# A fused two-block network: the filter network's first steps moved ahead of the projection, and five instead of one filling product in the routing

## The chip, the cores and the metric

The kernel runs on one core of one Trainium2 chip, in one launch. The metric is the device time of the launch in microseconds; the kernel before takes 2229.22 us (median of 3 runs). TensorE multiplies, VectorE and ScalarE do the elementwise work, SyncE and ScalarE issue the DMAs.

## The reference

Two hybrid layers (attention, RWKV-7, retention, feed-forward) are followed by a second block on 256 tokens of width 1024. Only the second block is touched. What matters of it, shortened:

```
h = rms_norm(x, g_mix) * (1 + sc1) + sh1
p = h @ w_in + b_in                                  # the projection, 1024 x 3600
q, k, v, o, gates, hx = split(p)
y_m  = mlstm_mixer(q, k, v, o, gates, ...)
filt = hyena_filters(256, w1, b1, w2, b2, w3, freq, deltas)
y_h  = hyena_mixer(hx, ..., filt, ...)
x = x + gt1 * (concatenate([y_m, y_h]) @ w_out)
hf = rms_norm(x, g_ffn) * (1 + sc2) + sh2
x = x + gt2 * expert_choice_moe(hf, w_router, w_gate, w_up, w_down)   # 16 experts, 32 tokens each

def hyena_filters(L, w1, b1, w2, b2, w3, freq, deltas):
    hid = sin(freq * (z @ w1 + b1))                  # z: 256 x 33, constant; 64 hidden units
    hid = sin(freq * (hid @ w2 + b2))
    return (hid @ w3) * (exp(-t * abs(deltas)) + 0.05)
```

The filters do not depend on `x`. The experts choose their tokens by a top-k of the router's softmax; the weights of an expert are 24 MB in 12 loads of 2 MB.

## The kernel before

Each engine has its own stream of instructions, written out by hand, with waits on semaphores between them. The projection of the second block is done in 16 tiles `q`; tile `q` uses columns of ring slot `n = q // 2` (three slots, loaded by SyncE). A tile writes bank `q % 2` of the accumulator PS and is copied out by ScalarE in `proj_out` (L1280; the gate rows, tiles 4 and 5, by L1273). Tiles 0 and 1 are plain products (L783, reached through `project` and `product`). Tiles of slots 1, 3, 4 to 7 are done in three rounds of products (`split_tile`, L796, L800, L804): ScalarE makes a rounded high part of the weights (`high_weights`, L1303) and of h (L1310, the tile `xh`), VectorE the low parts (`low_weights2`, L1450, and L1456, `xl`).

The filter network runs between these tiles. TensorE's `project_beside_filters` holds: tile 0; z @ w1 (L858, `f_hid` 1); tile 1; two unread products; hid @ w2 (L862, `f_hid` 2); tile 2; then four rounds of two filter tiles (hid @ w3, L842) and one tile each (tile 3; the gate rows, L816; tile 6; tile 7); then the spectra (L851). VectorE's `sine_argument` brings an argument into range in seven linked steps (L1432 to L1442, `f_arg`), ScalarE takes the sine (L1317, `f_sin`). VectorE takes the absolute value of the deltas once (L1459, `f_abs`), ScalarE makes the windows (L1289, `f_win`), and VectorE multiplies window and filter tile (L1466, `f_filt`). A filter tile `i` may be written only when `f_filt` stands at `i - 1`.

`unread(bank, times)` (L748) is a product of a constant with a constant that nobody reads; it costs TensorE time only and writes a bank that is free there.

The loads of the filter network are issued by ScalarE: small ones (`hyw1`, `hyw2`, and others) during the last feed-forward; the constants `c2` (1.9 MB, with z in it) at the start of the second block; then `filter_loads` (w3, two halves, L1264; the deltas, 1 MB, L1265). All of them count on the one semaphore `two_loaded`; the wait ahead of L858 is for 11 loads, which is all of them.

In the routing (`route`, `first_expert`) TensorE makes the router's logits (L1041), turns them (L1056) for VectorE's top-k (L1638 to L1642, ended by the copies to L1661), meanwhile does other products and one `unread(2)`, and then waits for the top-k in `index_row` (L1074). It goes on with the indices' products (L1068), the gather of the chosen tokens (L1082), and the experts' products: `hidden` (L1093, gate and up, one per 2 MB load) and `down_products` (L1109). SyncE issues the next 2 MB load (L667) each time such a product group frees its place; from then on to the end the 16 experts' weights are streamed.

Of the kernel before, what the change touches and what calls it, by code (L numbers as in the profile page):

```python
# [33 lines left out]
T = 256  # L34
# [227 lines left out]
def build(nc, io):  # L262

    ctx = ExitStack()
    with ctx:
# [11 lines left out]
        def sem(name):  # L277
            return ctx.enter_context(nc.semaphore(name))
# [209 lines left out]
        p2 = w_(16384, P2_N)  # L488
        hyw1, hyw2 = lora[0:33, 384:448], lora[0:64, 256:384]
        ARG, TRN = lora[:, 512:768], lora[:, 768:1024]  # L490
# [100 lines left out]
        def first_slot(m):  # L591
# [19 lines left out]
         expert_slots, xs_staged, ge_ready, hs_ready, he_ready, ht_ready, ht_out, ye_ready, scattered,  # L611
         vec2, out_done, place6, place7, h2_scaled, z_conv, extra_a_full, extra_b_full, extra_c_full, rows_made, rows_taken, part_sums, xh2_ready, xl2_ready, high2_ready, low2_ready) = (S[n] for n in names2)
        BASE2 = START + LAYERS * LAYER_BLOCKS
        FULL2 = 32 * LAYERS * LAYER_SLOTS // RING
# [120 lines left out]
        def second_tensor(pe):  # L735
# [9 lines left out]
            def unread(bank, times=1):  # L745

                for _ in range(times):
                    nt.matmul(PS[:, bank, 0:T], ones, con[:, 0:T], start=True, stop=True)  # L748
# [105 lines left out]
            def project_beside_filters():  # L854

                project(0, 1, 0)
                pe.wait_ge(two_loaded, 11 * 16)
                nt.matmul(PS[0:64, 3, 0:T], hyw1, c2[0:33, D_Z:D_Z + T], start=True, stop=True).then_inc(f_hid, 1)  # L858
                project(1, 2)
                unread(5, 2)  # L860
                pe.wait_ge(f_sin, 1)
                nt.matmul(PS[:, 3, T:2 * T], hyw2, ARG[0:64, :], start=True, stop=True).then_inc(f_hid, 1)  # L862
                project(2, 3)
                pe.wait_ge(f_sin, 2)
                for n in range(4):
                    filter_tiles(2 * n, 2 * n + 2)
                    project(BESIDE_FILTERS[n], BESIDE_FILTERS[n] + 1)
                pe.wait_ge(f_sum, 2)
                filter_spectra(0, 8)
# [164 lines left out]
            def route():  # L1034
# [26 lines left out]

                unread(2)
                pe.wait_ge(tok2_out, 4)
# [167 lines left out]
            token_sums(2, SQ1[:, 0:8:7, :]).then_inc(ss2, 1)  # L1231
            unread(5)
            pe.wait_ge(sq2, 2)
# [10 lines left out]
        def second_scalar(act):  # L1244
# [51 lines left out]

            act.dma_start(c2, io["constants_2"][:, 0:D_WORK]).then_inc(two_loaded, 16)
            def high_weights(n):

                s = n % RING  # L1300
                act.wait_ge(ring_full[s], FULL2 + 32 * (n // RING + 1))
                for i in range(4):
                    ins = na.activation(HIGH2[n][i].rearrange("p k c -> p (k c)"), ring[:, s, 1024 * i:1024 * (i + 1)], ACT.Copy)  # L1303
                ins.then_inc(high2_ready, 1)

            root(1)
            shifted()
            filter_loads()
            act.wait_ge(h2_ready, KD)
# [91 lines left out]
        def second_vector(dve):  # L1401
# [25 lines left out]
            def sine_argument(n):  # L1427
# [3 lines left out]
                arg, trn = ARG[rows, :], TRN[rows, :]  # L1431
                link(nv.tensor_scalar(arg, PS[rows, 3, T * n:T * (n + 1)], p2[rows, P2_HY + n:P2_HY + n + 1], p2[rows, P2_HY + 2:P2_HY + 3], ALU.add, ALU.mult))  # L1432
                big = 1.5 * 2.0 ** 23
# [19 lines left out]
            def filters():  # L1453
                lf = LF[0:H2]
                dve.wait_ge(xh2_ready, 1)
                nv.tensor_tensor(XL2[:, :, :], hT[:, :, :], XH2[:, :, :].bitcast(F32), ALU.subtract).then_inc(xl2_ready, 1)  # L1456
                low_weights2(1)
                dve.wait_ge(two_loaded, 11 * 16)
                nv.scalar_tensor_tensor(DELTA, DELTA, -1.0, DELTA, ALU.mult, ALU.max).then_inc(f_abs, 1)  # L1459
                sine_argument(0)  # L1460
                sine_argument(1)
                for i in range(8):
                    c, t, _ = filter_tile(i)
                    dve.wait_ge(f_h, i + 1)
                    dve.wait_ge(f_win, i + 1)
                    nv.scalar_tensor_tensor(FILT[:, t, c, :], WIN[:, i % 2, :], 0.05, PS[:, 4 + i % 2, :], ALU.add, ALU.mult).then_inc(f_filt, 1)  # L1466
                    if i == 1:
                        low_weights2(3)
                    elif i == 5:
                        dve.wait_ge(act2, 6)  # L1470
                        nv.scalar_tensor_tensor(lf, G4[0:H2, 1::2, :], -1.0, G4[0:H2, 1::2, :], ALU.mult, ALU.max).then_inc(gate_rows, 1)
                        conv(QK2, 0, P2_CQW, P2_CQB, 0, 4, 8)
# [943 lines left out]
        def _(act):  # L2416
# [246 lines left out]
            act.dma_start(wrt, io["router"]).then_inc(two_loaded, 16)  # L2663
            act.dma_start(hyw1, io["hy_w1_2"][0]).then_inc(two_loaded, 16)
            for half in range(2):
                act.dma_start(hyw2[:, 64 * half:64 * half + 64], io["hy_w2_2"][0]).then_inc(two_loaded, 16)
            na.activation(bias[:, 3:4], onec, ACT.Sqrt)
# [556 lines left out]
```

## Time and profile before

| | |
|---|---|
| median of 3 runs | 2229.22 us (2229.08 to 2229.65) |
| the profiled execution | 2227.82 us |
| its span | 2225.9 us |
| TensorE products busy in the span | 1888.0 us |
| VectorE, ScalarE busy | 956.5 us, 549.9 us |
| mean granted clock of TensorE | 0.917 of 2.4 GHz |
| bytes moved | 613.15 MB, mean 275 GB/s |

The span is divided among three stretches that matter here: the projection of the second block with the filter network (about 1090 to 1232 us), the rest of the mixer and the routing (to about 1318 us), and the experts (to the end). In the rows below a time is in us from the span's start; a row of a timeline has start, busy us, engine, line, operation, tiles, count, and in brackets how long the engine had been idle and what released it. One matmul of float32 appears as two records.

### The profile page before, as it was taken

Reading aid. Unit: us, or ns where it says so; the run is one execution under the profiler, and the core shown is the slowest. Engines: PE = TensorE matmul, PEld = TensorE weight load, DVE = VectorE, ACT = ScalarE, POOL = GpSimd, SP = SyncE. Lnnn points to the kernel's source line nnn. Section 1 sums busy time; section 2 is a strip of 40 time slices with the busy share of each in tenths; the row PEclk is TensorE's granted clock in tenths of the full one; section 3 lists DMA queues with packets and bytes.
Section 4 is the critical chain, followed back from the end, with each engine's and each line's share of the span. In section 5 each row is a group of like instructions: output and inputs, shape, how many; then the busy total and the mean of one; then the engine's idle time right before and its main releaser. Section 6 shows DMA issues by size and latency. Waiting matters only on the chain.

```text
span 2225.9 us, 28935 instructions
## 1 busy us (share of the span) xinstructions
PE 1888.0 (85%) x12562; PEld 1313.9 (59%) x12562; DVE 956.5 (43%) x1334; ACT 549.9 (25%) x580; POOL 30.2 (1%) x23
## 2 busy tenths in 40 slices
PE   7999999999999999999999999566666666666675
PEld 7998788888999878888769773121121212121211
DVE  6789458666769746865567630000000000000000
ACT  4555013443364302443354111000000000000001
POOL 0000010000000000000000000000000000000000
PEclk9999999999999999999999999878788878788868
DMA  7443734657443543565643579999999999999997
GB/s 255 174 157 117 256 114 152 199 156 219 174 163 141 189 181 114 189 190 156 197 152 114 202 308 427 428 427 428 428 429 428 429 428 428 429 428 428 429 428 326
DMA packets 189554, 613.15 MB, mean 275 GB/s; under 512 B 8332, under 2 KB 105100, under 8 KB 164236
## 3 DMA queue, kind: packets, MB, share of 16 engines
q1 hardware_dynamic: 186928, 602.04, 70.0%
q10 hardware_dynamic: 2524, 9.60, 1.2%
q8 instruction: 82, 1.34, 0.2%
q14 instruction: 20, 0.16, 0.0%
HBM read 610.57 MB, written 1.05 MB: 275 GB/s over the span
## 4 chain that ended last, share of the span: by engine, by line
PE 51%; DMA 35%; DVE 9%; ACT 2%; issue 1%; SPq 0%; ACTq 0%; DVEq 0%; PEldq 0%
DMA ring<-in_w_down 11%; DMA ring<-in_w_gate 11%; PE PS L1981 10%; DMA ring<-in_w_up 10%; PE PS L1982 5%; PE PS L1093 3%; PE PS L1886 3%; PE PS L1961 3%; PE PS L1954 3%; PE PS L1956 2%; DMA work<-in_w_down 2%; DVE ring_low L2705 1%; PE PS L1109 1%; PE PS L783 1%; PE PS L1868 1%
## 5 line engine op out<-in xcount | busy, mean ns | idle before, releaser
L1093 PE MATMUL PS<-work,proj 128*32 128x512 f32 x1024 | 155.0, 738 | 96.1 <-DMA work<-in_w_up 56.9
L1694 DVE TENSOR_TENSOR proj<-proj,PS 128x512 f32<-128x512 f32 x16 | 11.0, 688 | 495.3 <-PE PS L1093 495.3
L1981 PE MATMUL PS<-x_both,high_f 128*128 128x512 f32 x608 | 210.9, 396 | 0.0
L1982 PE MATMUL PS<-x_both,ring_low 128*128 128x256 f32 x704 | 195.6, 278 | 0.0
L1093 PE MATMUL PS<-ring,proj 128*32 128x512 f32 x768 | 126.7, 793 | 79.7 <-DMA ring<-in_w_up 41.0
L2688 DVE TENSOR_TENSOR ring_low<-ring,high_f 128x4096 fp32r<-128x4096 f32 (+1 forms) x38 | 146.8, 3863 | 27.8 <-ACT high_f L2437 27.7
L1093 PEld LDWEIGHTS PS<-work,proj 128*32 128x32 f32 x1024 | 31.2, 123 | 214.5 <-DMA work<-in_w_up 95.1
L2437 ACT ACTIVATE high_f<-ring 128x4096 fp32r<-128x4096 f32 (+1 forms) x38 | 121.1, 3188 | 114.5 <-PE PS L1982 90.3
L1385 ACT ACTIVATE proj<-PS 128x512 f32<-128x512 f32 x16 | 9.6, 597 | 518.3 <-PE PS L1093 518.2
L1982 PEld LDWEIGHTS PS<-x_both,ring_low 128*128 128x128 f32 x704 | 132.3, 188 | 0.0
L1981 PEld LDWEIGHTS PS<-x_both,high_f 128*128 128x128 f32 x608 | 114.2, 188 | 26.7
L1093 PEld LDWEIGHTS PS<-ring,proj 128*32 128x32 f32 x768 | 24.5, 128 | 175.2 <-DMA ring<-in_w_up 70.7
L1698 DVE TENSOR_TENSOR proj<-PS,xT 128x512 f32<-128x512 f32 x32 | 20.7, 687 | 223.7 <-PE PS L1109 207.1
L1981 PE MATMUL PS<-hid_both,high_f 128*128 128x512 f32 x308 | 106.9, 392 | 0.0
L1954 PE MATMUL PS<-xh_a,high_a 128*128 128x256 f32 x416 | 99.8, 283 | 0.0
L1956 PE MATMUL PS<-hT_low,high_a 128*128 128x256 f32 x400 | 96.8, 281 | 0.0
L1109 PE MATMUL PS<-work,proj 128*32 128x512 f32 x448 | 67.6, 735 | 25.5 <-DMA work<-in_w_down 22.7
L1982 PE MATMUL PS<-hid_both,ring_low 128*128 128x256 f32 x308 | 85.9, 279 | 0.0
L1387 ACT ACTIVATE proj<-PS 128x512 f32<-128x512 f32 x16 | 9.6, 597 | 295.6 <-PE PS L1101 295.6
L1142 PE MATMUL PS<-proj 128*128 128x512 f32 x128 | 62.5, 632 | 22.9 <-DVE proj L1698 22.9
L1109 PE MATMUL PS<-ring,proj 128*32 128x512 f32 x352 | 57.2, 782 | 29.0 <-DMA ring<-in_w_down 29.0
L1954 PEld LDWEIGHTS PS<-xh_a,high_a 128*128 128x128 f32 x416 | 77.3, 188 | 0.3 <-issue 0.2
(565 smaller groups left out, 3695.1 us busy)
## 6 DMA issues: line engine op xcount, KB each, us to landing
ring<-in_w_in SPq DMA_DIRECT2D x73, 1024.0 KB, 7.4
work<-in_w_gate SPq DMA_DIRECT2D x32, 2048.0 KB, 35.7
work<-in_w_up SPq DMA_DIRECT2D x32, 2048.0 KB, 35.5
work<-in_w_down SPq DMA_DIRECT2D x28, 2048.0 KB, 35.8
ring<-in_w_up SPq DMA_DIRECT2D x25, 2048.0 KB, 35.4
ring<-in_w_gate SPq DMA_DIRECT2D x23, 2048.0 KB, 35.4
ring<-in_w_down SPq DMA_DIRECT2D x22, 2048.0 KB, 36.3
ring<-in_w_ada SPq DMA_DIRECT2D x24, 1024.0 KB, 7.4
```

The source lines that it names most:

```text
L783: mm = nt.matmul(PS[0:m, q % 2, T * b:T * (b + 1)], weight(b, k), moving(k), start=(k == 0), stop=(k == kn - 1))
L1093: mm = nt.matmul(PS[32 * j:32 * j + 32, 2 + n // 4, :], x(k), w[:, F_E * kk + 512 * j:F_E * kk + 512 * (j + 1)], start=(k == 0), stop=(k = ...
L1109: mm = nt.matmul(PS[32 * c:32 * c + 32, 5 - dh, :], HTE[:, P * c + 32 * d:P * c + 32 * (d + 1)], w(D * c + 512 * dh), start=(d == 0), stop ...
L1142: return nt.matmul(PS[:, YB[2 * t + half], :], GE[:, P * t:P * (t + 1)], (YE, YE2)[half], start=False, stop=False, skip_group_check=True)
L1886: mm = nt.matmul(PS[:, bank(l, q), T * b:T * (b + 1)], weight(b, k), moving(k), start=(k == 0), stop=(k == kn - 1))
L1954: nt.matmul(out, h[:, c:c + P], high_x[:, k, :], start=(k == 0), stop=False)
L1956: nt.matmul(out, h[:, c:c + P], low_x[:, k, :], start=False, stop=False)
L1961: mm = nt.matmul(out, w[:, c:c + P], high_x[:, k, :], start=False, stop=(k == kn - 1 and not late))
L1981: nt.matmul(PS[:, at + b, :], h[:, c:c + P], both[:, k, :], start=(k == 0), stop=False, skip_group_check=True)
L1982: mm = nt.matmul(PS[:, at + b, 0:T], w[:, c:c + P], both[:, k, 0:T], start=False, stop=(k == kn - 1), skip_group_check=True)
L2437: na.activation(high(n)[:, w], ring[:, n % RING, w], ACT.Copy).then_inc(high_ready, 1)
L2688: nv.tensor_tensor(ring_low[:, n % RING, c], w, high(n)[:, c].bitcast(F32), ALU.subtract).then_inc(low_dve, 1)
```

## The change

Seven edits, all in the second block or just ahead of it:

- z gets a tile of its own, `features` (33 x 256, in `lora`), loaded by ScalarE with `hyw1` and `hyw2` during the last feed-forward; these four loads count on a new semaphore `features_loaded`.
- z @ w1 moves from behind tile 0 to the place of one unread product ahead of tile 0; it and the later steps use bank 4 instead of 3.
- The two unread products behind tile 1 are gone.
- The wait for the big loads (now 8 on `two_loaded`) moves behind tile 2 on TensorE, and behind the second sine argument on VectorE.
- `filter_loads` is issued right behind `c2`, ahead of the root of the norm and the shift of h (`root(1)`, `shifted()`).
- VectorE: first sine argument ahead of `xl`; the deltas behind the second argument; the low parts of slot 3 behind filter tile 3 instead of 1.
- Routing: `unread(2)` becomes `unread(2, 5)`.

```diff
@@ project_beside_filters (TensorE)
                 project(0, 1, 0)
-                pe.wait_ge(two_loaded, 11 * 16)
-                nt.matmul(PS[0:64, 3, 0:T], hyw1, c2[0:33, D_Z:D_Z + T], start=True, stop=True).then_inc(f_hid, 1)
                 project(1, 2)
-                unread(5, 2)
                 pe.wait_ge(f_sin, 1)
-                nt.matmul(PS[:, 3, T:2 * T], hyw2, ARG[0:64, :], start=True, stop=True).then_inc(f_hid, 1)
+                nt.matmul(PS[:, 4, T:2 * T], hyw2, ARG[0:64, :], start=True, stop=True).then_inc(f_hid, 1)
                 project(2, 3)
+                pe.wait_ge(two_loaded, 8 * 16)
                 pe.wait_ge(f_sin, 2)
@@ route (TensorE)
-                unread(2)
+                unread(2, 5)
                 pe.wait_ge(tok2_out, 4)
@@ second_tensor, start
             token_sums(2, SQ1[:, 0:8:7, :]).then_inc(ss2, 1)
-            unread(5)
+            pe.wait_ge(features_loaded, 4 * 16)
+            nt.matmul(PS[0:64, 4, 0:T], hyw1, features, start=True, stop=True).then_inc(f_hid, 1)
             pe.wait_ge(sq2, 2)
@@ second_scalar (ScalarE)
             act.dma_start(c2, io["constants_2"][:, 0:D_WORK]).then_inc(two_loaded, 16)
+            filter_loads()
...
             root(1)
             shifted()
-            filter_loads()
             act.wait_ge(h2_ready, KD)
@@ filters (VectorE)
+                sine_argument(0)
                 dve.wait_ge(xh2_ready, 1)
                 nv.tensor_tensor(XL2[:, :, :], hT[:, :, :], XH2[:, :, :].bitcast(F32), ALU.subtract).then_inc(xl2_ready, 1)
                 low_weights2(1)
-                dve.wait_ge(two_loaded, 11 * 16)
+                sine_argument(1)
+                dve.wait_ge(two_loaded, 8 * 16)
                 nv.scalar_tensor_tensor(DELTA, DELTA, -1.0, DELTA, ALU.mult, ALU.max).then_inc(f_abs, 1)
-                sine_argument(0)
-                sine_argument(1)
                 for i in range(8):
...
-                    if i == 1:
+                    if i == 3:
                         low_weights2(3)
@@ the small loads (ScalarE, during the last feed-forward)
-            act.dma_start(hyw1, io["hy_w1_2"][0]).then_inc(two_loaded, 16)
+            act.dma_start(hyw1, io["hy_w1_2"][0]).then_inc(features_loaded, 16)
+            act.dma_start(features, io["constants_2"][0:33, D_Z:D_Z + T]).then_inc(features_loaded, 16)
             for half in range(2):
-                act.dma_start(hyw2[:, 64 * half:64 * half + 64], io["hy_w2_2"][0]).then_inc(two_loaded, 16)
+                act.dma_start(hyw2[:, 64 * half:64 * half + 64], io["hy_w2_2"][0]).then_inc(features_loaded, 16)
```

TensorE's stream at the start of the second block, before (a row is line, operation, tiles written and read, shape, count; `con` is the constants, L742 the token sums, L753 the token rows, L783 tiles 0 and 1, L796 the first round of tile 2):

```order
L748 MATMUL PS<-con 128x256 x2
L742 MATMUL PS<-con,proj 128x64 x4
L748 MATMUL PS<-con 128x256
L753 MATMUL PS<-con,stat 128x128 x2
L748 MATMUL PS<-con 128x256 x2
L783 MATMUL PS<-hT,ring 128x256 x16
L858 MATMUL PS<-work,lora 64x256
L783 MATMUL PS<-hT,ring 128x256 x16
L748 MATMUL PS<-con 128x256 x2
L862 MATMUL PS<-lora 128x256
L796 MATMUL PS<-xh_71,high_1_0_73 128x256 x2
```

and now (lines below 610 have moved by a few; L1232 is z @ w1, L860 hid @ w2, L784 tiles 0 and 1):

```order
L749 MATMUL PS<-con 128x256 x2
L743 MATMUL PS<-con,proj 128x64 x4
L1232 MATMUL PS<-lora 64x256
L754 MATMUL PS<-con,stat 128x128 x2
L749 MATMUL PS<-con 128x256 x2
L784 MATMUL PS<-hT,ring 128x256 x32
L860 MATMUL PS<-lora 128x256
L797 MATMUL PS<-xh_71,high_1_0_73 128x256 x2
```

The small product stands where an unread one stood, tiles 0 and 1 follow each other without anything between them, and hid @ w2 follows tile 1 at once.

VectorE's stream behind the scaling of h, before, from the end of the low parts of slot 1 to the low parts of slot 3 (the steps L1436 to L1440 of both arguments left out; L1459 is the deltas, L1466 the filter products):

```order
L1450 TENSOR_TENSOR ring_low<-ring,high_1_3_76 128x1024
L1459 SCALAR_TENSOR_TENSOR work<-work 128x2048
L1432 TENSOR_SCALAR lora<-PS,work 64x256
...
L1432 TENSOR_SCALAR lora<-PS,work 128x256
...
L1466 SCALAR_TENSOR_TENSOR work<-proj,PS 128x512 x2
L1450 TENSOR_TENSOR ring_low<-ring,high_3_0_77 128x1024
...
L1466 SCALAR_TENSOR_TENSOR work<-proj,PS 128x512 x4
```

and now, from the scaling of h on:

```order
L1754 SCALAR_TENSOR_TENSOR hT<-xT,small,PS 128x256 x8
L1432 TENSOR_SCALAR lora<-PS,work 64x256
...
L1457 TENSOR_TENSOR xl_72<-hT,xh_71 128x2048
...
L1432 TENSOR_SCALAR lora<-PS,work 128x256
...
L1461 SCALAR_TENSOR_TENSOR work<-work 128x2048
L1466 SCALAR_TENSOR_TENSOR work<-proj,PS 128x512 x4
L1450 TENSOR_TENSOR ring_low<-ring,high_3_0_77 128x1024
...
L1466 SCALAR_TENSOR_TENSOR work<-proj,PS 128x512 x2
```

The first argument has moved ahead of `xl`, the deltas behind the second argument, and four instead of two filter products stand ahead of the low parts of slot 3.

TensorE's stream in the routing, now, from the turned logits to the first expert's first product (L1055, L1092):

```order
L1055 MATMUL PS<-con,proj 16x128 x2
L1047 MATMUL PS<-con,proj 128x128 x8
L1023 MATMUL PS<-con,xT 128x128 x8
L749 MATMUL PS<-con 128x256 x5
L1073 MATMUL PS<-proj,con 128x64
L1067 MATMUL PS<-con,proj 128x16 x2
L1081 MATMUL PS<-cond,proj 128x64 x8
L1092 MATMUL PS<-tri,proj 32x512 x8
```

Five unread products (before: one, L748) now stand between the residual's products and the index row that waits for the top-k.

## Rows read from the trace of the kernel before

**Rows 1.** The chain that ended last, in order of time, from the experts on

```profile
1360.64 13.91 PE PS L1093 x128
1374.78 34.06 DMA ring<-in_w_gate
```

**Rows 2.** Timeline, start of the second block to filter tile 0

```profile
1089.80 0.35 ACTq L1297 DMA_DIRECT2D work<-in_constants  x1
...
1091.83 0.26 ACT L1250 ACTIVATE stat<-PS,bias 128x2 f32<-128x2 f32 x1 [13.85 <-PE PS L742]
...
1094.06 7.14 PE L783 MATMUL PS<-hT,ring 128*128 128x256 f32 x32 [0.34 <-ACT hT L1256]
...
1097.32 0.60 ACTq L1265 DMA_DIRECT2D work<-in_hy_deltas  x1
...
1104.27 0.64 PE L858 MATMUL PS<-work,lora 33*64 33x256 f32 x2 [3.07 <-DMA work<-in_hy_deltas]
...
1104.84 8.86 PE L783 MATMUL PS<-hT,ring 128*128 128x256 f32 x32
...
1110.45 0.53 DVE L1432 TENSOR_SCALAR lora<-PS,work 64x256 f32<-64x256 f32 x1
...
1113.20 0.42 ACT L1317 ACTIVATE lora<-lora 64x256 f32<-64x256 f32 x1 [7.51 <-DVE lora L1442]
...
1115.12 1.21 PE L796 MATMUL PS<-xh,high 128*128 128x256 f32 x8
...
1120.98 1.13 PE L842 MATMUL PS<-work,lora 64*128 64x512 f32 x4
```

**Rows 3.** Timeline, from the gate rows to the last filter tiles

```profile
1128.96 3.64 PE L816 MATMUL PS<-hT,ring 128*4 128x256 f32 x64
...
1129.95 4.63 DVE L1450 TENSOR_TENSOR ring_low<-ring,high 128x1024 fp32r<-128x1024 f32 x4 [4.58 <-ACT high L1303]
...
1132.67 1.90 ACT L1273 ACTIVATE proj<-PS,work 4x256 f32<-4x256 f32 x4 [2.03 <-PE PS L816]
1134.50 1.28 DVE L1466 SCALAR_TENSOR_TENSOR work<-proj,PS 128x512 f32<-128x512 f32 x2
...
1135.24 1.81 PE L842 MATMUL PS<-work,lora 64*128 64x512 f32 x4 [2.64 <-DVE work L1466]
...
1136.98 2.07 PE L796 MATMUL PS<-xh,high 128*128 128x256 f32 x8
...
1144.24 1.13 PE L842 MATMUL PS<-work,lora 64*128 64x512 f32 x4
```

**Rows 4.** Timeline, routing and first expert

```profile
1313.53 0.60 PE L748 MATMUL PS<-con 128*128 128x256 f32 x2
...
1317.05 0.40 PE L1074 MATMUL PS<-proj,con 16*128 16x64 f32 x2 [2.93 <-DVE proj L1661]
...
1317.87 3.67 PE L1082 MATMUL PS<-cond,proj 128*128 128x64 f32 x16
...
1321.47 3.39 PE L1093 MATMUL PS<-tri,proj 128*32 128x512 f32 x16
...
1324.79 2.10 PE L1082 MATMUL PS<-cond,proj 128*128 128x64 f32 x16
...
1327.76 3.58 PE L1093 MATMUL PS<-ring,proj 128*32 128x512 f32 x16
...
1356.94 3.70 PE L1142 MATMUL PS<-proj 128*128 128x512 f32 x8 [1.48 <-DVE proj L1698]
```

**Rows 5.** Windows: busy time by engine, then TensorE's granted clock, DMA share, GB/s

```profile
1106.00:1109.00 3.00, 3.00 (x8) 2.36 (x8) 3.00 (x4) 0.00 (x0) 0.00 (x0) 0.50 0.00 0
1137.00:1140.00 3.00, 3.00 (x15) 3.00 (x15) 2.96 (x8) 0.00 (x0) 0.00 (x0) 0.50 1.05 386
1318.00:1336.00 18.00, 18.00 (x110) 9.59 (x114) 2.79 (x7) 0.17 (x1) 0.00 (x0) 0.73 0.86 303
1340.00:1360.00 20.00, 16.93 (x131) 6.02 (x124) 1.98 (x3) 4.78 (x5) 0.00 (x0) 1.00 1.01 429
```

More of the change, by code:

```diff
@@ L488, in build @@
         p2 = w_(16384, P2_N)
-        hyw1, hyw2 = lora[0:33, 384:448], lora[0:64, 256:384]
+        hyw1, hyw2, features = lora[0:33, 384:448], lora[0:64, 256:384], lora[0:33, 0:T]
         ARG, TRN = lora[:, 512:768], lora[:, 768:1024]
@@ L612, in build @@
          vec2, out_done, place6, place7, h2_scaled, z_conv, extra_a_full, extra_b_full, extra_c_full, rows_made, rows_taken, part_sums, xh2_ready, xl2_ready, high2_ready, low2_ready) = (S[n] for n in names2)
+        features_loaded = sem("features_loaded")
         BASE2 = START + LAYERS * LAYER_BLOCKS
@@ L1431, in sine_argument @@
                 arg, trn = ARG[rows, :], TRN[rows, :]
-                link(nv.tensor_scalar(arg, PS[rows, 3, T * n:T * (n + 1)], p2[rows, P2_HY + n:P2_HY + n + 1], p2[rows, P2_HY + 2:P2_HY + 3], ALU.add, ALU.mult))
+                link(nv.tensor_scalar(arg, PS[rows, 4, T * n:T * (n + 1)], p2[rows, P2_HY + n:P2_HY + n + 1], p2[rows, P2_HY + 2:P2_HY + 3], ALU.add, ALU.mult))
                 big = 1.5 * 2.0 ** 23
```

## The prediction

> **What bounds the kernel now.** I read the chain that ended last first. From 1374.78 us on it is loads of expert weights with short products between them, to the end [rows 1], and the DMA engines are full long before that: 429 GB/s between 1340 and 1360 [rows 5]. The experts' bytes are fixed, so the end stands where this stream starts, plus a constant. Ahead of it the loads are let go by TensorE's and VectorE's progress, so whatever shortens the second block's projection, mixer or routing moves the start of the stream, and the end with it. The question is therefore how much sooner TensorE gets through, and whether the stream follows.
>
> The timeline shows the places. In the first, tile 0 ends at 1094.06 + 7.14 = 1101.20; the product z @ w1 waits 3.07 us for the last big load, the deltas; tile 1 then takes 8.86 us where tile 0, the same sixteen products, took 7.14 [rows 2]. The windows say why: the granted clock is 0.50, the 1.2 GHz level, between 1106 and 1109 [rows 5], after an engine that stood still. In the second, TensorE ends the gate rows at 1128.96 + 3.64 = 1132.60 and stands 2.64 us for the filter products that free its banks; VectorE was busy until 1129.95 + 4.63 = 1134.58 with the low parts of slot 3 [rows 3]. Again the clock falls to 0.50, in 1137 to 1140 [rows 5]. In the third, in the routing, the one unread product ends at 1313.53 + 0.60 = 1314.13 and TensorE waits 2.93 us for the top-k; the first gather then takes 3.67 us where the second, equally long, takes 2.10, and the experts' first two groups take 3.39 and 3.58 [rows 4], where eight such groups in a row take 13.91 / 8 = 1.74 each [rows 1].
>
> **The change part by part.** The sum is made against the profiled execution, 2227.82 us, 1.4 below the median of 2229.22; I take the same difference off both.
>
> Tile 0 to tile 2. Before: 1101.20 to 1115.12 [rows 2], 13.92 us, which hold the wait (3.07), z @ w1, tile 1 at a clock partly halved, two unread products, and hid @ w2. After: tile 1 at the full clock, 7.14, and hid @ w2, for which I take the 0.64 of z @ w1, the nearest row; 7.78 in all. Gain 6.1 us. Ends that overlap the next product may add 0.3. Who must be ready: the sine for hid @ w2 stands on ScalarE behind h's high part, slot 1's high parts, tile 0's copy and a table load. ScalarE had done all of them by 1113.20 - 7.51 = 1105.7 and idled for the argument [rows 2]; TensorE now comes for the sine at 1101.20 + 7.14 = 1108.3, 2.6 us behind. The argument takes VectorE 1113.20 - 1110.45 = 2.8 us [rows 2] behind the scaling of h, while ScalarE still makes h's high part, for which VectorE must wait anyway; if none of it were covered, slot 1's low parts would end 2.8 us later, and tile 2 needs them only after its first two rounds. The second argument needs 2.8 us and a sine of 0.42 behind hid @ w2; tile 2 covers it with 1120.98 - 1115.12 = 5.86 us [rows 2]. If that cover were gone it would cost those 3.2 us.
>
> z @ w1 itself stands where an unread product stood and costs 0.64 against 0.60 [rows 2, 4]: nothing. Its four small loads are issued before ScalarE's idle 13.85 us ahead of the root [rows 2], so with that much cover at least; the extra issue, 0.60 if it is like the deltas', falls into that idle time: nothing.
>
> The three big issues ahead of the root. They begin when c2's issue ends, 1089.80 + 0.35, and take three times 0.60 at most: 1091.95, against 1091.83 for the root [rows 2]. Loss 0.1 us; behind ScalarE's root wait the reciprocal, the token rows and the scaling of h, all on the path. If c2's issue came later, at most 1.8.
>
> The filter products. With the low parts of slot 3 behind filter tile 3, the banks for tiles 4 and 5 are free in time: the windows and filter products of tiles 2 and 3 need only what follows tile 2. What is late next is the copy of the gate rows, which the next tile waits for: ScalarE ends it 1132.67 + 1.90 - 1132.60 = 2.0 us behind TensorE's gate rows [rows 3]. The two filter tiles fill 1.1 of that, and about 1 us is a new wait. Before, 1136.98 - 1132.60 = 4.4 us passed there; after, 2.1. Gain 2.3 us. Slot 3's low parts now end about together with that copy, and tile 6 needs them only behind its first two rounds of products.
>
> Tile 6 at the full clock: 5.9 us (as tile 2) instead of 1144.24 - 1136.98 = 7.3 [rows 3]. Gain 1.4 us, if a wait of 1 us does not bring the clock down. The nearest row: a wait of 1.48 us at 1356.94 [rows 4] left it at 1.00 [rows 5].
>
> The sum to here is 6.1 - 0.1 + 2.3 + 1.4 = 9.7 us. The deltas' load is issued about 6 us earlier (1091.4 instead of 1097.3) and first waited for behind tile 2; I expect no wait for it.
>
> The routing. Four more unread products at 7.14 / 16 = 0.45 us [rows 2] fill 1.8 of the 2.93 us; the top-k still sets the end of the wait, which is 1.1 us, shorter than the 1.48 that left the clock alone. If so, gather and both groups run at the full clock: 3.67 - 2.10 = 1.6, 3.39 - 1.74 = 1.65, 3.58 - 1.74 = 1.85, together 5.1 us of TensorE [rows 1, 4]. Of this the end gets what the DMA engines had stood idle: between 1318 and 1336 they moved 303 GB/s times 18 us = 5.45 MB instead of 429 times 18 = 7.72 [rows 5], so 5.3 us of the stream were lost. About 1.5 us of that I leave (an estimate: the engines are empty when the indices free the first load at about 1317.5, and it takes time to arrive). Then a load is 2.1 MB / 429 = 4.9 us; the first group would free its place at 1317.87 + 2.10 + 1.74 = 1321.7, 4.2 us behind, the second some 5 us later, and the stream does not run dry. Gain 5.3 - 1.5 = 3.8 us, bounds 0 (the clock falls as before) and 5.1.
>
> Sum: 9.7 + 3.8 = 13.5 us. Profiled 2214.3, median 2229.22 - 13.5 = 2215.7 us.
>
> A page stands against the two clock terms. The Trainium skill, "TensorE: Matmul & The Clock Gate", section "What's actually happening", says that the chip's look at TensorE's activity runs freely, not tied to the kernel, so that the number of slow products varies from run to run. By that the two falls could come at another place after every shift. The rows bear it out little: the three runs of before lie within 0.57 us, less than one such fall costs. It is the second and third of the cases below.
>
> **The rivals.** (1) The forecast, 2215.7, own range 2213.5 to 2217: 0.60. (2) The routing's clock falls all the same, since the 1.1 us wait is followed by small products (16 rows, 64 columns) that load TensorE little; for it: the clock fell again at 1328 in before, with no wait worth naming, the second group at 3.58 [rows 4]; against it: the 1.48 us wait. 2215.7 + 3.8 = 2219.5; if only the second group falls, the stream loses under 1 us and it counts to the forecast. Chance 0.15. (3) The new wait ahead of tile 6 halves the clock there: 2217.1. Chance 0.10. (4) A new wait eats part of the front: the low parts of slot 1 behind the first argument, or the copies that now come in denser order; a slip of 3 to 5 us, 2219 to 2221. Every margin I found is 2.5 us or more. Chance 0.07. (5) The stream does not follow: if loads ahead of the routing, not TensorE, set when the experts begin, the 9.7 us become a longer wait and only 3.8 or less are left, 2225.4 or more. Against it: the chain has products, not loads, through the routing, and the loads wait for TensorE. Chance 0.05. (6) Slower: z @ w1 now stands ahead of the norm's token rows, and behind it on TensorE the whole block. If the small loads (33 rows of z, issued while ring loads run) were late by more than the 13.5 us gained, plus the 4.5 of the bound, it would be slower than 2233.7; with 13.85 us of cover this needs a landing time of some 32 us, while the 1 MB of the deltas, issued at 1097.32, let TensorE go at 1104.27 [rows 2]. Chance 0.02; with 0.01 for the change that does nothing because something else holds tile 1.
>
> **How the numbers follow.** 0.2% is 4.5 us, about what a measurement of this kernel tells from no change: faster is below 2224.8. Cases 1 to 4 are there, 0.92, and most of what is left of 5 lies on the edge: faster 0.94, within 0.04, slower 0.02. The range takes in cases 1, 2, 3 and the nearer part of 4, and the upper bounds of the gain (0.3 and 1.3 more): 2213.0 to 2220.0.
>
> **What the profile would show.** z @ w1 (L1232) with no wait for a load; tiles 0 and 1 as one run of about 14 us with clock 1.00; filter tiles 4 and 5 directly behind the gate rows, then about 1 us of idle time ahead of tile 6, released by L1273; the last filter tiles about 9.7 us earlier than 1144.24; in the routing a wait of about 1.1 us ahead of L1073, the first gather near 2.1, and above 400 GB/s from 1320 us less the shift on. Wrong it would be with a clock of 0.50 in any of the three places, with a wait of hid @ w2 for the sine, or with the routing 9.7 us earlier and the end not.

## The result and the profile after

| | before | changed |
|---|---|---|
| median | 2229.28 us (2228.98 to 2231.51, 6 runs) | 2216.06 us (2214.74 to 2219.06, 6 runs) |
| ratio | | 0.9939, 95% interval 0.993 to 0.9949 |
| the profiled execution, its span | 2227.82, 2225.9 us | 2219.06, 2217.1 us |

The change makes the kernel 13.2 us faster; 13.5 were forecast (2215.7 us). The profiled execution of the changed kernel is the slowest of its six, and its own difference is only 8.8 us of span. Both facts need an explanation, and the trace has one. This is the timeline of the first stretch after (columns as in [rows 2]; lines have moved: L1232 is z @ w1, L784 tiles 0 and 1, L860 hid @ w2, L797 a first round, L843 filter tiles, L817 the gate rows):

```profile
1091.12 0.35 ACTq L1297 DMA_DIRECT2D work<-in_constants  x1
1091.50 1.13 ACTq L1264 DMA_DIRECT2D work<-in_hy_w  x2
1092.66 0.71 ACTq L1265 DMA_DIRECT2D work<-in_hy_deltas  x1
1093.04 0.64 PE L1232 MATMUL PS<-lora 33*64 33x256 f32 x2
1093.42 0.26 ACT L1250 ACTIVATE stat<-PS,bias 128x2 f32<-128x2 f32 x1 [13.59 <-PE PS L743]
...
1095.64 14.05 PE L784 MATMUL PS<-hT,ring 128*128 128x256 f32 x64 [0.34 <-ACT hT L1256]
...
1106.06 0.42 ACT L1317 ACTIVATE lora<-lora 64x256 f32<-64x256 f32 x1
1109.62 0.70 PE L860 MATMUL PS<-lora 64*128 64x256 f32 x2
...
1110.25 1.22 PE L797 MATMUL PS<-xh,high 128*128 128x256 f32 x8
...
1124.11 3.64 PE L817 MATMUL PS<-hT,ring 128*4 128x256 f32 x64
...
1127.67 1.13 PE L843 MATMUL PS<-work,lora 64*128 64x512 f32 x4
1127.81 1.91 ACT L1273 ACTIVATE proj<-PS,work 4x256 f32<-4x256 f32 x4 [2.02 <-PE PS L817]
...
1129.82 1.17 PE L797 MATMUL PS<-xh,high 128*128 128x256 f32 x8 [1.02 <-issue]
...
1135.63 1.13 PE L843 MATMUL PS<-work,lora 64*128 64x512 f32 x4
```

The first row shows where to begin: c2's issue, the first instruction of the second block on ScalarE, stands at 1091.12 us, against 1089.80 before [rows 2]. The only thing that the change adds ahead of it is the early load of z, and it is not the reason: the two small issues ahead of that load already stand 1.32 us apart (before, then after):

```profile
1073.73 0.33 ACTq L2662 DMA_DIRECT2D cond<-in_constants  x1
```

```profile
1075.05 0.34 ACTq L2662 DMA_DIRECT2D cond<-in_constants  x1
```

In the fourteen profiles of this study c2's issue stands anywhere from 1089.80 to 1092.30: 1089.80 to 1091.46 in the four kernels without the early load of z, 1090.02 to 1092.30 in the ten profiles with it. So I read the second block from c2's issue on. Then tiles 0 and 1 are one run of 14.05 us and nothing is waited for until tile 6, where 1.02 us pass; TensorE needs the sine at 1109.62 and it was ready at 1106.06 + 0.42. The last filter tiles begin at 1135.63 - 1091.12 = 44.51 us, where it was 1144.24 - 1089.80 = 54.44 [rows 2, 3]: 9.93 us sooner.

The routing after:

```profile
1304.90 2.32 PE L749 MATMUL PS<-con 128*128 128x256 f32 x10
...
1308.43 0.40 PE L1073 MATMUL PS<-proj,con 16*128 16x64 f32 x2 [1.20 <-DVE proj L1661]
...
1309.20 2.10 PE L1081 MATMUL PS<-cond,proj 128*128 128x64 f32 x16
...
1311.23 1.93 PE L1092 MATMUL PS<-tri,proj 128*32 128x512 f32 x16
1313.09 2.10 PE L1081 MATMUL PS<-cond,proj 128*128 128x64 f32 x16
...
1316.06 1.92 PE L1092 MATMUL PS<-ring,proj 128*32 128x512 f32 x16
```

Against [rows 4] the wait ahead of the index row is 1.20 instead of 2.93 us, and gathers and groups run at the full clock. The windows after (columns as in [rows 5]); the third is the 18 us behind the issue of the load that the indices free, at 1309.27, and the last lies in the tail:

```profile
1106.00:1109.00 3.00, 3.00 (x16) 2.64 (x15) 2.69 (x3) 0.46 (x2) 0.00 (x0) 1.00 0.00 0
1309.00:1315.00 6.00, 6.00 (x51) 4.43 (x50) 1.15 (x4) 0.20 (x1) 0.00 (x0) 1.00 0.80 284
1309.27:1327.30 18.03, 18.03 (x150) 9.56 (x154) 2.90 (x8) 1.22 (x2) 0.00 (x0) 1.00 0.95 380
2201.00:2206.00 5.00, 4.19 (x12) 1.38 (x12) 1.38 (x2) 0.94 (x3) 0.00 (x0) 0.50 0.02 6
```

The stream moved 380 GB/s there, where it had been 303 [rows 5]. The first wait of the chain for a full stream comes after this row:

```profile
1361.42 36.15 DMA ring<-in_w_gate
```

TensorE reached that wait 1361.42 - 1308.43 = 52.99 us behind the index row, where it had been 1374.78 - 1317.05 = 57.73 [rows 1, 4]: 4.74 us sooner. But the wait itself grew from 34.06 to 36.15 us, so 2.65 us of it are left at its end. And the end of the chain, first before, then after:

```profile
2208.54 3.64 PE PS L1136 x16
2212.95 1.98 PE PS L1142 x4
```

```profile
2197.47 3.69 PE PS L1135 x16
2201.93 3.78 PE PS L1141 x4
```

From the index row to the last but one group of the last expert (L1136, then L1135) it took 2208.54 - 1317.05 = 891.49 us before and 2197.47 - 1308.43 = 889.04 after. From there to the end it took 17.36 us before and 19.63 after: the granted clock was 0.50 over the last scatter but one (3.78 instead of 1.98 us), in a piece of program that the change does not touch. The profiled difference is then whole: 1.32 (start) - 9.94 (front, to the index row) - 2.45 (routing and stream) + 2.27 (tail) = -8.80 us. The front is the change. Of the 2.45 us only a part may be, as the experiments show. The start differs between executions of one kernel (1091.12 and 1092.30 us in the two profiles of the changed kernel). For the tail this is not shown: that scatter took 3.78 us in both profiles of the changed kernel, and in seven of the fourteen profiles in all, among them routing_only, which has the front of before. Whether the slow tail belongs to the execution or to the changed kernel stays open.

### The profile page after: what moved, and what is told of

Read it like the earlier page. It is cut to its first block, busy times and chain, and to the rows that moved or that the text cites. A ratio compares the mean times of both kernels' runs of the same rounds, so it can differ in the third digit from the quotient of the medians.

```text
span 2217.1 us, 28941 instructions
## 1 busy us (share of the span) xinstructions
PE 1878.2 (85%) x12564; PEld 1310.5 (59%) x12564; DVE 956.4 (43%) x1334; ACT 549.8 (25%) x580; POOL 30.2 (1%) x23
## 4 chain that ended last, share of the span: by engine, by line
PE 53%; DMA 35%; DVE 9%; ACT 2%; issue 1%; ACTq 0%; SPq 0%; DVEq 0%; PEldq 0%
PE PS L1981 10%; DMA ring<-in_w_up 10%; DMA ring<-in_w_gate 10%; DMA ring<-in_w_down 10%; PE PS L1982 5%; PE PS L1886 3%; PE PS L1092 3%; PE PS L1961 3%; PE PS L1954 3%; PE PS L1956 3%; DMA work<-in_w_down 2%; DMA work<-in_w_gate 2%; DMA work<-in_w_up 2%; PE PS L1108 1%; PE PS L784 1%; DVE ring_low L2706 1%
## 5 line engine op out<-in xcount | busy, mean ns | idle before, releaser
L1092 PE MATMUL PS<-work,proj 128*32 128x512 f32 x1024 | 154.6, 737 | 99.9 <-DMA work<-in_w_up 60.0
L1092 PE MATMUL PS<-ring,proj 128*32 128x512 f32 x768 | 121.1, 762 | 80.1 <-DMA ring<-in_w_up 45.2
L1092 PEld LDWEIGHTS PS<-work,proj 128*32 128x32 f32 x1024 | 31.0, 122 | 217.3 <-DMA work<-in_w_up 97.1
L1092 PEld LDWEIGHTS PS<-ring,proj 128*32 128x32 f32 x768 | 24.0, 125 | 172.2 <-DMA ring<-in_w_up 73.4
L1108 PE MATMUL PS<-ring,proj 128*32 128x512 f32 x352 | 55.8, 764 | 32.4 <-DMA ring<-in_w_down 32.4
```

The source lines that it names most:

```text
L1092: mm = nt.matmul(PS[32 * j:32 * j + 32, 2 + n // 4, :], x(k), w[:, F_E * kk + 512 * j:F_E * kk + 512 * (j + 1)], start=(k == 0), stop=(k = ...
L1108: mm = nt.matmul(PS[32 * c:32 * c + 32, 5 - dh, :], HTE[:, P * c + 32 * d:P * c + 32 * (d + 1)], w(D * c + 512 * dh), start=(d == 0), stop ...
```

## The experiments

Each kernel was timed beside the kernel before on the same chip; the medians of before were 2229.5 to 2230.74 there, so ratios are compared and not medians. A ratio of 0.001 is 2.2 us. With these intervals, some 3 us either way at worst, a single microsecond is not told by the times. It is told by the profile, by three spans that the start and the tail leave alone: c2's issue to the last filter tiles, c2's issue to the index row, index row to the first of the last expert's final two groups (L1135 or L1136). Even these are one profile each. routing_only has the front of before and needed 0.47 us more to the filter tiles; the front of the changed kernel, which waits for no load there, repeated to 0.06 us over five profiles.

| kernel | ratio (95%) | to filter tiles | to index row | index row to last weights |
|---|---|---|---|---|
| before | 1 | 54.44 | 227.25 | 891.49 |
| changed | 0.9939 (0.993 to 0.9949) | 44.51 | 217.31 | 889.04 |
| changed, again | 0.9947 (0.9934 to 0.9961) | 44.49 | 217.29 | 888.61 |
| routing_only | 0.9999 (0.999 to 1.0008) | 54.91 | 227.70 | 888.72 |
| front_only | 0.9951 (0.9938 to 0.9964) | 44.50 | 217.28 | 890.70 |
| loads_only | 0.9993 (0.9985 to 1.0002) | 55.18 | 227.99 | 890.70 |
| lows_only | 0.9983 (0.9974 to 0.9991) | 49.86 | 222.67 | 889.40 |
| vector_order_back | 0.9969 (0.9957 to 0.9981) | 50.42 | 223.24 | 891.10 |
| loads_back | 0.9938 (0.9925 to 0.9951) | 44.26 | 217.06 | 888.70 |
| gates_first | 0.9938 (0.9926 to 0.9951) | 43.48 | 216.28 | 891.07 |
| gates_first_loads_back | 0.9933 (0.9919 to 0.9947) | 43.19 | 216.02 | 889.42 |
| fill_three | 0.9952 (0.9938 to 0.9966) | 44.52 | 217.32 | 894.51 |
| fill_nine | 0.9945 (0.9933 to 0.9957) | 44.55 | 217.80 | 890.13 |
| unread_kept | 0.9946 (0.9932 to 0.9959) | 45.34 | 218.15 | 890.32 |

### Front and routing apart

```diff
 (routing_only: before with)
-                unread(2)
+                unread(2, 5)
 (front_only: the changed kernel with)
-                unread(2, 5)
+                unread(2)
```

> The kernel before with five unread products instead of one in the routing, nothing else. Theory (the clock is held and the stream of expert weights starts without gaps): TensorE's wait ahead of the index row falls from 2.93 to about 1.2 us, the granted clock stays at 1.00 over the first gather and the first two expert groups (gather 2.1 instead of 3.67 us, groups 1.9 instead of 3.39 and 3.58), and the end moves by what the changed kernel's stream gained, 2.6 us (2226.7 against 2229.3). Rival 1 (my prediction's size for this term): 3.8 us. Rival 2 (the clock falls all the same, or the later stream makes up for it): within 0.5 us of before.

> The changed kernel with the one unread product of before in the routing. Theory (the terms add up): the front alone gives 9.9 us, so about 2219.4, with the routing again at a clock of 0.50 and its first gather at 3.6 us. Rival (the clock's phase has moved with the shift, so the routing's fall is gone even without the extra products): 2217 or less, with the gather at 2.1 us. Rival (the front's gain is absorbed later): 2222 or more.

The front alone holds nearly everything: 0.9951, 10.9 us (8.0 to 13.8), and 9.97 us sooner at the index row. The routing alone is not told from nothing by the time, 0.2 us (2.2 faster to 1.8 slower), although its profile shows the mechanism whole, with a wait of 1.20, a gather of 2.10 and groups of 1.92 us, and 888.72 us to the last weights. In front_only the clock fell as in before:

```profile
1308.92 0.40 PE L1073 MATMUL PS<-proj,con 16*128 16x64 f32 x2 [2.92 <-DVE proj L1661]
1309.70 3.53 PE L1081 MATMUL PS<-cond,proj 128*128 128x64 f32 x16
1313.16 3.64 PE L1092 MATMUL PS<-tri,proj 128*32 128x512 f32 x16
1316.73 2.10 PE L1081 MATMUL PS<-cond,proj 128*128 128x64 f32 x16
...
1319.70 1.92 PE L1092 MATMUL PS<-ring,proj 128*32 128x512 f32 x16
```

Here the second group ran at the full clock, which it had not in before [rows 4], and the stretch took 890.70 us, 0.8 less than before with the very same instructions. So of the 2.45 us between the two profiles a part belongs to the execution.

### The loads alone, and VectorE's order alone

```diff
 (loads_only: before with)
             act.dma_start(c2, io["constants_2"][:, 0:D_WORK]).then_inc(two_loaded, 16)
+            filter_loads()
...
             root(1)
             shifted()
-            filter_loads()
 (vector_order_back: the changed kernel with)
-                sine_argument(0)
                 dve.wait_ge(xh2_ready, 1)
...
-                sine_argument(1)
                 dve.wait_ge(two_loaded, 8 * 16)
                 nv.scalar_tensor_tensor(DELTA, DELTA, -1.0, DELTA, ALU.mult, ALU.max).then_inc(f_abs, 1)
+                sine_argument(0)
+                sine_argument(1)
```

> The kernel before with the three big loads of the filter network issued ahead of the root of the norm, nothing else; z @ w1 still waits for all 11 loads behind tile 0. Theory (on TensorE the wait for the deltas hides a second one: VectorE's order, in which the argument stands behind xl, slot 1's low parts and the deltas): the wait ahead of z @ w1 goes, tile 1 runs at the full clock, and TensorE then waits 3 to 4 us for the sine ahead of hid @ w2; gain 0 to 1.5 us. Rival (the late load was the whole cost of this place): hid @ w2 comes 4.5 us earlier, gain 4 to 5 us. Rival (the delay of the root counts most): 0.3 us slower.

> The changed kernel with VectorE's order of before for the sine arguments (behind xl, slot 1's low parts and the deltas), all else changed. Theory (VectorE's order was a second bound that lay hidden under the wait for the deltas): TensorE waits for the sine ahead of hid @ w2 by some 4 to 5 us, and of the 6.3 us that the first place gave about 5 are lost, so 2216.1 + 5 = 2221, more if the clock falls behind that wait. Rival (my prediction's accounting, in which the place's cost was the wait for the load and the clock behind it): no more than 1 us lost, 2217.

In loads_only none of the three things came that my theory named: the wait for the deltas did not go, tile 1 did not run at the full clock, and TensorE did not wait for the sine. The time is not told from before (1.6 us faster; from 3.3 faster to 0.4 slower). Its profile:

```profile
1093.01 0.65 ACTq L1265 DMA_DIRECT2D work<-in_hy_deltas  x1
...
1105.33 0.82 PE L858 MATMUL PS<-work,lora 33*64 33x256 f32 x2 [2.26 <-DMA work<-in_hy_deltas]
1106.09 8.63 PE L783 MATMUL PS<-hT,ring 128*128 128x256 f32 x32
...
1115.51 0.70 PE L862 MATMUL PS<-lora 64*128 64x256 f32 x2
```

The deltas were issued at 1093.01, 1.55 us behind c2 (1091.46) instead of 7.5 us behind it, and TensorE was let go at 1105.33: 13.9 us behind c2, against 14.5 (1104.27 - 1089.80, [rows 2]). An issue 6 us earlier brought the release 0.6 us forward in this pair of profiles, which is less than it differs among executions with the late issue: lows_only was let go 13.5 us behind c2, routing_only 14.9. The clock fell again (8.63 us for tile 1), and the last filter tiles came 0.7 us later than before.

vector_order_back shows what had stood under that wait:

```profile
1112.91 1.15 PE L860 MATMUL PS<-lora 64*128 64x256 f32 x2 [4.35 <-ACT lora L1317]
...
1120.94 1.13 PE L843 MATMUL PS<-work,lora 64*128 64x512 f32 x4
```

With z @ w1 early and the loads out of the way, but the argument still behind the low parts and the deltas, TensorE waits 4.35 us for the sine, and the clock falls behind it (0.57 in 1113 to 1117), so that tile 2 ends 8.0 us after hid @ w2 began, not 6.5. Of the 9.9 us of the front 5.9 are gone, and in time 6.7 of 13.6 (ratios 0.9969 and 0.9939). Filter tile 0 began 1120.94 - 1090.05 = 30.89 us behind c2, where it was 31.18 before [rows 2]: without VectorE's order the first place gained 0.3 us, and the 4.0 that are left of the front are nearly all the low parts' edit (3.7, next section). The theory of a hidden second bound stands; the accounting by which this place cost a wait for a load and the clock behind it falls.

### The low parts of slot 3 alone

```diff
-                    if i == 1:
+                    if i == 3:
                         low_weights2(3)
```

> The kernel before with the low parts of slot 3 behind filter tile 3 instead of 1, nothing else. Theory (the low parts held up the banks, then the clock fell): the 2.64 us wait ahead of filter tile 4 goes, about 1 us of a new wait stands ahead of tile 6, the clock is not 0.50 over tile 6, gain 2.3 + 1.4 = 3.7 us (2225.6). Rival (the new wait brings the clock down as well): 2.3 us or less. Rival (tile 6 then waits for the low parts): under 1 us.

Measured: 0.9983, 3.8 us (2.0 to 5.8), 3.7 expected.

```profile
1103.35 0.64 PE L858 MATMUL PS<-work,lora 33*64 33x256 f32 x2 [2.06 <-DMA work<-in_hy_deltas]
1103.92 7.17 PE L783 MATMUL PS<-hT,ring 128*128 128x256 f32 x32
1113.74 0.70 PE L862 MATMUL PS<-lora 64*128 64x256 f32 x2 [1.79 <-ACT lora L1317]
...
1133.92 1.19 PE L796 MATMUL PS<-xh,high 128*128 128x256 f32 x8 [1.01 <-issue]
...
1139.75 1.13 PE L842 MATMUL PS<-work,lora 64*128 64x512 f32 x4
```

The filter tiles are 4.58 us sooner. 3.7 of it lie behind tile 2 and are the edit's: the wait ahead of tile 6 is 1.01 us, tile 6 takes 1139.75 - 1133.92 = 5.83 us. The rest is this execution's: its wait for the deltas was 2.06 us, the clock did not fall, tile 1 took 7.17 us, and yet hid @ w2 began only 0.85 us sooner after c2, since it then waited 1.79 us for the sine. That is the second bound again, seen in the order of before.

### What is left: the loads' place, the gate rows, the unread products

```diff
 (loads_back: filter_loads() behind shifted() again)
 (gates_first)
-        BESIDE_FILTERS = [3, 4, 6, 7]
+        BESIDE_FILTERS = [4, 3, 6, 7]
-                    sp.wait_ge(block_done, BASE2 + 2 * (n - RING + 1))
+                    sp.wait_ge(block_done, BASE2 + (6 if n == 4 else 2 * (n - RING + 1)))
-                    act.wait_ge(block_done, BASE2 + q + 1)
+                    act.wait_ge(block_done, BASE2 + (6 if q == 3 else q + 1))
 (unread_kept: unread(5, 2) behind project(1, 2) again)
 (fill_three, fill_nine: unread(2, 3), unread(2, 9) in route)
```

> The changed kernel with the three big loads issued behind the shift of h again, as before. Theory (with z in a small tile of its own, nothing needs the big loads until behind tile 2; their early issue gains nothing and delays the root): the root comes 0.25 us sooner after c2's issue (2.03 instead of 2.30 us), no wait for the deltas anywhere, and the time is the same within the noise or 0.3 us less. Rival (the early issue is needed): a wait ahead of filter tile 0 or of the windows, 1 us or more slower.

> The changed kernel with the gate rows computed ahead of tile 3 instead of behind it (ring slot 1 is then let go by tile 3, and its next load issued, after both). Theory (the 1.02 us of idle time ahead of tile 6 is the copy of the gate rows, and nothing else): the wait goes, filter tile 6 begins 1.0 us sooner after c2's issue (43.5 instead of 44.5 us), 2215.1. Rival (another wait takes its place, for slot 3's low parts or its high parts): no gain.

> The changed kernel with both edits: the gate rows ahead of tile 3, and the big loads issued behind the shift of h. Theory (the two are independent): 1.0 + 0.25 us less than the changed kernel, about 2214.8 against its 2216.1. Rival (the later loads are then needed sooner than they land): the gain of the one is lost.

> The changed kernel with the two unread products kept behind tile 1. Theory (they stand on the path, nothing waits at that place): hid @ w2 begins 0.9 us later after c2's issue, and filter tile 6 too, 2217.0. Rival (they were needed for the clock): tile 2 is faster with them than the 5.9 us without, and no loss.

The spans to the index row bear all four theories out (each is one profile): 217.06, 216.28, 216.02 and 218.15 us against 217.31, that is 0.25, 1.03 and 1.29 us sooner and 0.84 later. Once z has its own tile, the early issue of the big loads is a small loss. The 1 us ahead of tile 6 was the copy of the gate rows. The times point to gates_first_loads_back as the fastest (0.9933), but its interval holds the changed kernel's ratio too; that it beats it is not shown by the times. In gates_first's profile the clock fell over the routing, and the later span was 2 us longer (891.07), so the 1 us gained in front did not reach the end there.

> The changed kernel with nine unread products in the routing. Theory: they end 0.6 us behind the top-k (nine times 0.43 against the 3.5 us that were free), so the index row comes 0.6 us later after the first logit turned, the clock is 1.00 as with five; 0.6 us slower than with five, or the same where the stream hides it. Rival (only the clock counts and five are too few in some executions): up to 1 us faster than with five.

> The changed kernel with three unread products in the routing. Theory (what brings the clock down is how long TensorE stands ahead of the index row): a wait of 2.93 - 2 * 0.45 = 2.0 us; the clock may fall or not (it fell behind waits of 2.6 and more, did not behind 1.8 and 1.5), so the end lies between that with one (2218.7) and with five (2216.1). Rival (the number of products does not matter at all for the end): the same as with one.

> The changed kernel itself, once more, for a second profiled execution and a second set of times. Theory (whether TensorE's clock falls in the routing, with five unread products as with one, differs from execution to execution): the front is as in the first profile to 0.1 us (index row 217.3 us after c2's issue), but the durations of the first gathers and expert groups differ from the first profile's, some at half the clock, and the time from the index row to the last expert's last weights is 0 to 2 us longer than 889.0 us. Rival (the five products hold the clock in this kernel, and the falls seen in its variants come from their own order): gather 2.10 us and groups 1.92 again, 889.0 us.

With nine the index row comes 0.49 us later, where 0.6 were expected, and the first groups are at the full clock, but the second took 3.44 us. With three the wait was 2.06 us and the clock stayed down for longest of all, over both gathers and both groups, 894.51 us:

```profile
1308.15 0.66 PE L1073 MATMUL PS<-proj,con 16*128 16x64 f32 x2 [2.06 <-DVE proj L1661]
1309.51 3.67 PE L1081 MATMUL PS<-cond,proj 128*128 128x64 f32 x16
1313.12 3.64 PE L1092 MATMUL PS<-tri,proj 128*32 128x512 f32 x16
1316.69 3.68 PE L1081 MATMUL PS<-cond,proj 128*128 128x64 f32 x16
```

With five the clock was held in both profiles of the changed kernel and in routing_only. In the variants with five it was not: the first gather took 3.44 us in vector_order_back, 3.14 in gates_first, 2.68 in loads_back, 2.53 in gates_first_loads_back, all behind the same wait of 1.2 us; in unread_kept the first group took 3.59. loads_back's routing rows are the same instructions in the same order as the changed kernel's, and the index row stood within 0.1 us of the same time from the span's start (1308.47 and 1308.43):

```profile
1308.47 0.40 PE L1073 MATMUL PS<-proj,con 16*128 16x64 f32 x2 [1.18 <-DVE proj L1661]
...
1309.25 2.68 PE L1081 MATMUL PS<-cond,proj 128*128 128x64 f32 x16
1311.85 2.92 PE L1092 MATMUL PS<-tri,proj 128*32 128x512 f32 x16
```

My last expectation was that the changed kernel itself would show such falls in a second execution. It did not: 2.10 and 1.92 us again, 888.61 us. Two executions of one kernel, and one each of the others, do not tell whether the execution or the kernel decides. That stays open.

What the fourteen profiles do show is what such a fall costs. Add up the busy time of the four pieces (first gather, first group, second gather, second group) and set it beside the span from the index row to the last weights:

| four pieces, us | profiles | index row to last weights |
|---|---|---|
| 8.0 (full clock) | changed, changed again, routing_only | 888.61 to 889.04 |
| 9.6 | loads_back, lows_only, gates_first_loads_back, fill_nine | 888.70 to 890.13 |
| 11.2 | front_only, loads_only, unread_kept, gates_first, vector_order_back | 890.32 to 891.10 |
| 12.7 | before | 891.49 |
| 14.4 | fill_three | 894.51 |

The span grows with the slow time, whatever the number of unread products; the first 1.6 us of slow time cost the end between nothing and 1.3 us. The products only move a kernel up or down this table, and not reliably: the four profiles with one product stand at 9.6, 11.2, 11.2 and 12.7, the eight with five at 8.0 three times, at 9.6 twice and at 11.2 three times. The mean span is 890.6 us with one and 889.6 with five.

## Why the prediction was right, point by point

- **The total.** Forecast 13.5 us, measured 13.2 (11.4 to 15.6), and in changed_again 11.8 (8.7 to 14.7). That the first came within 0.3 us is partly luck: the front gave a little more than forecast, the routing clearly less, and the first place gave its size only because an edit that had no price of its own was among the seven.
- **The bound.** Right. From the end of the first stream wait (1408.88 before, 1397.61 after) to TensorE's product at 2074.57 and 2063.25 the chain took 665.69 and 665.64 us, and the end followed the front.
- **Tile 0 to tile 2, gain 6.1.** Measured from the start of tile 0: 1115.12 - 1094.06 = 21.06 us before, 1110.25 - 1095.64 = 14.61 after, 6.45. The size is right; I had allowed 0.3 for overlap, and it was 0.35 more than 6.1. The reading of where it came from, "the wait (3.07), z @ w1, tile 1 at a clock partly halved", was incomplete: the end of the place was held by VectorE's order as well, only about 1 us behind. Without that edit vector_order_back gained 1.84 us up to hid @ w2 (22.86 us behind c2 instead of 24.70) and, since the clock then fell, 0.3 up to filter tile 0. I had costed the argument's move only as something that must be ready, not as a term that the gain depends on.
- **The big issues ahead of the root, loss 0.1.** c2's issue to tile 0 is 4.52 instead of 4.26 us; 0.26, and 0.25 came back in loads_back. I had noted the loads' earlier issue without a price or a gain; the runs give it a small loss and no gain.
- **The filter products, gain 2.3, and tile 6, gain 1.4.** From the end of the gate rows to tile 6: 1129.82 - 1127.75 = 2.07 us where 2.1 were forecast, and 5.81 us for tile 6 where 5.9 were. lows_only confirms both alone, and gates_first confirms the cause that was named for the 1 us left.
- **The routing, gain 3.8.** The term that was mis-sized. The steps came as forecast (a wait of 1.20, all four pieces at the full clock, more than 400 GB/s soon after), and yet the stretch to the last weights is 2.45 us shorter, not 3.8. TensorE's own gain was close to the forecast, 4.7 us of 5.1; what failed is how much of it the end gets. The bytes of the 18 us window would give (380 - 303) * 18.03 / 428 = 3.2 us. Up to the end of the first stream wait before moved 402 GB/s over 90.87 us, 36.5 MB, and after 418 over 88.30, 36.9 MB: 0.4 MB more, or 0.9 us of the stream. So part of the bytes that came sooner were not those of the load that was waited for. Nor does this one pair of profiles size the term: the mean over the profiles with one and with five products differs by 1.0 us only. In the times it is 0.2 us in routing_only (2.2 faster to 1.8 slower) and 2.7 us as the difference of the changed kernel (0.9 with changed_again) and front_only, none clear of noise. Rival 2, that the clock falls all the same, had 0.15; with six of nine profiles with five or nine extra products showing a fall in one of the four pieces, it deserved more.
- **The clock behind the new 1 us wait** (rival 3) did not fall in any profile that has this wait.
- **The slow stretches that shift between runs** (cases two and three). The last scatter but one, the second group and tile 1 ran at either level behind the same instructions. The Trainium skill, "TensorE: Matmul & The Clock Gate", section "What's actually happening", says that the number of slow products varies from run to run of one kernel. The rows fit it across kernels; the one kernel that was profiled twice does not show it (2.10 and 1.92 in the routing, 3.78 in the tail, both times). I had given this little weight because of the narrow spread of three runs; in the comparisons of this study the runs of before spread over 5 to 9 us, of which up to 2.5 are the start of the second block.

## What to carry to other kernels

When a wait is to be removed, look at what the next instruction behind it waits for and when that would have been ready: here the second wait lay 1 us behind the first, and only the edit of another engine's order made the first worth removing. Give a small early operand its own tile and its own semaphore; issuing the big loads behind which it used to hide sooner brought nothing. Measure small edits between two marks in the trace on either side of them; start, tail and clock of an execution move the total by more than the edit does.

## What the runs showed of the hardware

- An issue 6 us earlier brought the landing of the deltas only about 1 us forward. In the nine profiles that issue them 1.5 us behind c2 they landed 13.0 to 13.9 us behind c2 (mean 13.5), in the five that issue them 7.5 us behind it 13.5 to 15.0 (mean 14.5). Windows of loads_only and then of before:

```profile
1096.00:1098.00 2.00, 2.00 (x10) 1.76 (x11) 1.98 (x6) 2.00 (x6) 0.00 (x0) 1.00 0.95 396
1098.00:1102.00 4.00, 4.00 (x20) 3.54 (x19) 1.45 (x1) 3.97 (x5) 0.00 (x0) 1.00 1.03 260
```

```profile
1096.00:1098.00 2.00, 2.00 (x11) 1.76 (x10) 0.11 (x1) 0.74 (x3) 0.00 (x0) 1.00 0.31 92
1098.00:1104.00 6.00, 3.20 (x15) 2.47 (x13) 2.59 (x2) 6.00 (x7) 0.00 (x0) 1.00 0.73 242
```

  The gap in the engines' work was filled, but the rest of c2, w3 and the deltas (these last one row of HBM to 128 partitions) then moved at 260 GB/s with the engines fully busy, where the expert weights reach 429. Which of the three loads is the slow one no run tells.
- How long TensorE stood did not decide whether its clock fell: 2.06 us ahead of z @ w1 left it at full speed in lows_only, 2.06 us ahead of the index row brought it to half in fill_three, and 1.2 us ahead of it was followed by a fall at the first gather in four profiles, at the first group in one, and by none in three.
